# Sparse attention as one stream of steps: later PV products, an earlier compressed branch, top-k in pieces, full-height masks

## The reference

```python
# compressed branch: 127 compressed keys; its probabilities also rate the 32 blocks of 64 keys
s_c = einsum('btgrd,bngd->bgrtn', q_g, k_cmp) * ATTN_SCALE
p_c = _masked_softmax(s_c, end_pos <= pos)
o_c = einsum('bgrtn,bngd->btgrd', p_c, v_cmp)
imp = einsum('bgtn,nj->bgtj', sum(p_c, axis=2), overlap)
score = where(forced, inf, where(causal, imp, -inf))
sel_val, sel_idx = top_k(score, 16)       # 16 of 32 blocks for each query and group
# selected branch: softmax over the keys of the chosen blocks; window branch: the last 512 keys
o = g[..., 0:1] * o_c + g[..., 1:2] * o_s + g[..., 2:3] * o_w
# FoX: causal softmax attention with a forget bias, 16 heads
y = sigmoid(g_a) * (o_nsa @ w_up_nsa) + sigmoid(g_b) * (o_fox @ w_up_fox)
```

## Time and profile before

| what | us |
|---|---|
| median of 3 runs | 9327.44 |
| lowest and highest of them | 9312.08, 9807.5 |
| the profiled execution | 9306.09 |
| its span on the slowest core (core 5) | 9304.6 |
| spans of the 8 cores | 9266.1 to 9304.6 |
| mean granted TensorE clock of core 5 | 0.960 of full speed |
| PE busy over the span | 8538.8 |

### The profile page before, as it was taken

The page is one execution under the profiler, slowest core; times in us unless marked ns, Lnnn a source line. Parts: engine busy times, 40 slices in busy tenths (PEclk is TensorE's granted clock), DMA queues, the critical chain, the costliest instruction groups (busy, mean ns, idle before and its releaser), DMA issues.

```text
span 9304.6 us, 111637 instructions; the slowest of 8 cores (9266.1 to 9304.6 us)
## 1 busy us (share of the span) xinstructions
PE 8538.8 (92%) x42959; PEld 3887.5 (42%) x42959; DVE 1613.7 (17%) x3493; ACT 1743.1 (19%) x2961; POOL 355.5 (4%) x676
## 2 busy tenths in 40 slices
PE   1279999999998888888889999999999999999999
PEld 0134444444444543333334444444444444444444
DVE  2233113110001112222222223111101111111111
ACT  1134323221005652222220013000000000000000
POOL 0000000000000000000000000000000000000000
PEclk7589999999999999999989999999999999999999
DMA  9963678788623331222225566446545654564465
GB/s 193 171 147 80 111 127 152 146 147 150 119 55 78 83 85 39 56 53 43 52 56 114 116 153 135 81 95 152 124 77 114 151 110 75 128 154 93 77 141 126
DMA packets 334602, 1014.58 MB, mean 109 GB/s; under 512 B 81056, under 2 KB 138816, under 8 KB 248832
## 3 DMA queue, kind: packets, MB, share of 16 engines
q0 software_dynamic: 96768, 700.33, 42.8%
q1 hardware_dynamic: 237312, 307.10, 10.2%
HBM read 1573.38 MB, written 134.22 MB: 184 GB/s over the span
## 4 chain that ended last, share of the span: by engine, by line
PE 85%; DMA 6%; DVE 4%; issue 2%; ACT 2%; DVEq 0%; SPq 0%; ACTq 0%; POOLq 0%
PE ps L339 84%; DMA xt_25_67<-xT 1%; DMA ws_43<-w_ada 1%; DMA ws_46<-w_ada 1%; DMA xt_26_68<-xT 1%; PE ps L343 1%; DMA xt_27_69<-xT 1%; DVE of_78_120 L353 0%; DMA cx_46_88<-xT 0%; DVE onsa_140 L359 0%; DVE oaccS_139 L353 0%; DVE oaccS_139 L359 0%; ACT pT_74_116 L346 0%; ACT pT_76_118 L346 0%; ACT pT_75_117 L346 0%
## 5 line engine op out<-in xcount | busy, mean ns | idle before, releaser
L339 PE MATMUL ps<-hown_61,ws_43 128*128 128x512 bf16 x2816 | 718.9, 392 | 3.0 <-DMA ws_43<-w_inF 3.0
L339 PE MATMUL ps<-hown_61,ws_45 128*128 128x512 bf16 x2816 | 717.6, 393 | 0.0
L339 PE MATMUL ps<-hown_61,ws_44 128*128 128x512 bf16 (+1 forms) x2688 | 690.4, 394 | 0.0
L346 ACT ACTIVATE rl_138_180<-ps 128x512 f32<-128x512 f32 x128 | 76.4, 597 | 2118.5 <-PE ps L339 2118.5
L339 PEld LDWEIGHTS ps<-hown_61,ws_45 128*128 128x128 bf16 x2816 | 265.9, 101 | 272.8 <-issue 59.3
L339 PEld LDWEIGHTS ps<-hown_61,ws_43 128*128 128x128 bf16 x2816 | 264.5, 100 | 271.8 <-issue 58.6
L339 PEld LDWEIGHTS ps<-hown_61,ws_44 128*128 128x128 bf16 (+1 forms) x2688 | 255.4, 101 | 257.5 <-issue 58.6
L339 PE MATMUL ps<-hown_61,ws_46 128*128 128x512 bf16 x1472 | 344.1, 388 | 0.0
L339 PE MATMUL ps<-x1T_164,ws_45 128*128 128x512 bf16 x1408 | 309.4, 380 | 13.1 <-DVE x_132_174 L359 13.1
L339 PE MATMUL ps<-x1T_164,ws_43 128*128 128x512 bf16 x1408 | 307.6, 379 | 0.0
L339 PE MATMUL ps<-uT_179,ws_44 128*128 128x512 bf16 x1408 | 307.5, 379 | 0.0
(11 more groups left out here) (453 smaller groups left out, 9909.1 us busy)
## 6 DMA issues: line engine op xcount, KB each, us to landing
ws_44<-w_ada POOLq DMA_DIRECT2D x53, 1024.0 KB, 10.5
ws_46<-w_ada POOLq DMA_DIRECT2D x48, 1024.0 KB, 10.7
ws_43<-w_ada POOLq DMA_DIRECT2D x46, 1024.0 KB, 10.7
ws_45<-w_ada POOLq DMA_DIRECT2D x45, 1024.0 KB, 11.5
ws_43<-w_inF POOLq DMA_DIRECT2D x44, 1024.0 KB, 9.0
ws_45<-w_inF POOLq DMA_DIRECT2D x44, 1024.0 KB, 8.5
ws_45<-w_ff POOLq DMA_DIRECT2D x43, 1024.0 KB, 8.8
ws_43<-w_ff POOLq DMA_DIRECT2D x43, 1024.0 KB, 9.7
```

Source lines behind the costliest of these rows:

```text
L339: S.emit(PE, lambda e: e.matmul(out_, lhsT, rhs, start=start, stop=stop, skip_group_check=True), reads, writes)
L346: S.emit(ACT, lambda e: e.activation(out=out_, in_=in_, func=func, **kw), reads, writes)
```

## The change

All three branches of a group become one generator of steps, `group(g)`, and one loop drives it. In each step the loop writes the score and mask products and the exponential, then up to three pieces from a list `todo`, then the PV of the step before last (`LAG = 2`), whichever branch that step belongs to, and at a branch's end its work on DVE (`post`). The compressed branch of the next tile stands between the window and the selected branch of this one. The eight top-k operations, the transpose to `selT` and its copy, and the transposes of `onsa` wait in `todo`. `selT` has 128 rows (96 of them zero), as have the compressed keys, so every mask product contracts over 128 partitions. `FILL_N` gives 430 ns of GEMM to a step, and 1000 (window, selected) or 2200 (compressed) plus another 430 after a branch's last PV. There are two `oacc` tiles, four `pq` tiles and two `selT` tiles; the next 256 queries are loaded two tiles ahead. In FoX `fin` is put back by one more step. The transposes go to bank 7 of PSUM instead of bank 4, and the modulation work that used this bank is drained before the stage. The total of products is the same but for the height of the masks. In the diff, cut to its core, the `post` shown is that of the compressed branch, and the last `todo.extend` is that of the selected one, whose `out_` transposes `onsa`; the NSA lines that these replace stand in the kernel above.

```diff
-                    pend.append(fin)
+                    pend.append(lambda: pend.append(fin))
...
+            def scores(s_, n, k, kb, q4, masks):
+                out_ = s_.t[:, 0:4 * n].rearrange("p (r t) -> p r t", r=4)
+                mm(out_, k, q4[0], True, not masks, [kb, q4[1]], [s_.b])
+                for i, (a, b, rd) in enumerate(masks):
+                    mm(out_, a, rep4(b), False, i == len(masks) - 1, rd, [s_.b])
...
+                def post():
+                    smt = weights(n, q0, g, 0)
+                    oa = oacc[q0] = oar.next()
+                    for r in range(4):
+                        p, c0 = oap(r)
+                        if r == 0:
+                            ts(DVE, imp.t[0:n], p.t[0:n, c0 + 129:c0 + 161], smt.t[0:n, 4:5], None, ALU.mult, None,
+                               [smt.b], [imp.b, p.b])
+                        else:
+                            stt(imp.t[0:n], p.t[0:n, c0 + 129:c0 + 161], smt.t[0:n, 4 + r:5 + r], imp.t[0:n],
+                                ALU.mult, ALU.add, [smt.b], [imp.b, p.b])
+                        ts(DVE, oa.t[0:n, r, :], p.t[0:n, c0:c0 + 128], smt.t[0:n, r:r + 1], None, ALU.mult, None,
+                           [smt.b], [oa.b, p.b])
+                    j = 32 * QT.index((q0, n))
+                    sT = selT[q0] = selTs.next()
+                    todo.extend([
+                        lambda: tt(DVE, sc.t[0:n], imp.t[0:n], ftab.t[0:n, j:j + 32], ALU.add, [imp.b, ftab.b], [sc.b]),
...
+                        None, None,
+                        lambda: tr(PtB[0:32, 512:512 + n], sbb.t[0:n, 0:32], ident[0:n, 0:n], [sbb.b, cb.b], [Pt.b]),
+                        lambda: cp(DVE, sT.t[0:32, 0:n], PtB[0:32, 512:512 + n], [], [sT.b, Pt.b]),
+                        lambda: ready.add(q0)])
+                    return 2200
...
+                    todo.extend([None] * 5 + [out_])
...
+            load_q(0)
+            yield from comp(*QT[0])
+            for i, qt in enumerate(QT):
+                for j, (t0, _) in enumerate(QL):
+                    if t0 == qt[0]:
+                        load_q(j + 1)
+                yield from window(*qt)
+                if i + 1 < len(QT):
+                    yield from comp(*QT[i + 1])
+                else:
+                    yield None
+                yield from selected(*qt)
...
+                    s_, pT = Rst.next(), pq.next()
+                    s(s_)
...
+                run_todo(3)
+                if len(pend) > LAG or (step == "end" and pend):
+                    pv, pT, post = pend.pop(0)
+                    pv(pT)
+                    if post is not None:
+                        yield FILL_N + (post() or 1000)
+                yield FILL_N
```

More of the change, by code:

```diff
@@ L19 @@
 QOFF = NK - TOWN
+QT = [(128 * i, 128) for i in range(8)]
+QL = [(256 * i, 256) for i in range(4)]
 SCALE = 128 ** -0.5
@@ L977, in nsa @@
         kwT = ZN.tile("kwT", [128, NK], BF16)
[L978 removed]
+        ZN = Bump(M, o_misc, o_aend)
         ca = ZN.tile("ca", [128, NCA], BF16)
[L980 to L982 removed]
+        ftab = ZN.tile("ftab", [128, 32 * len(QT)], F32)
+        vs = ZN.tile("vs", [128, NK // 128, 130], BF16)
+        vw = ZN.tile("vw", [128, NK // 128, 130], BF16)
         q4r = ZN.ring("q4", 2, [128, 4, 256], BF16)
[L984 to L985 removed]
+        pq = ZN.ring("pq", 4, [128, 512], BF16)
+        oar = ZN.ring("oacc", 2, [128, 4, 128], F32)
         onsa = ZN.tile("onsa", [128, 4, 128], BF16)
[L987 removed]
+        smr = ZN.ring("sm", 4, [128, 12], F32)
         imp = ZN.tile("imp", [128, 32], F32)
@@ L995, in nsa @@
         sbb = ZN.tile("sbb", [128, 32], BF16)
-        selT = ZN.tile("selT", [32, 128], BF16)
+        selTs = ZN.ring("selT", 2, [128, 128], BF16)
         dma(POOL, ca.t[:], ca_d, [], [ca.b])
         dma(SP, ftab.t[:], ftab_d, [], [ftab.b])
-        memset(vs.t[:, :, 128:130], 1.0, vs.b)
-        memset(vw.t[:, :, 128:130], 1.0, vw.b)
+        for v in (vs, vw):
+            memset(v.t[:, :, 128:130], 1.0, v.b)
+        for v in selTs.items:
+            memset(v.t[:], 0.0, v.b)
         memset(vcmp.t[:, :, 128:129], 1.0, vcmp.b)
@@ L1002, in nsa @@
         cp(DVE, vcmp.t[:, :, 129:161], rep4(ca.t[:, CA_OV:CA_OV + 32]), [ca.b], [vcmp.b])
-        cmpb = ca.t[:, CA_CMPB:CA_CMPB + 1024]
         Rst = Ring(PS[0:2])
         OA = PS[2:4]
[L1006 to L1013, removed]
+        Pt = PS[7]
+        PtB = PSB[id(Pt)]
+        LAG = 2
@@ L1014, in weights, with oap @@
+        todo = []
+        def oap(r):
+            return OA[r // 2], 256 * (r % 2)
+        def weights(n, q0, g, br):
+            smt = smr.next()
             for b in range(2):
-                ts(DVE, smt.t[:, 8 + 2 * b:10 + 2 * b], OA[b].t[:, 128:385:256], 1e-30, None, ALU.max, None, [],
+                ts(DVE, smt.t[0:n, 8 + 2 * b:10 + 2 * b], OA[b].t[0:n, 128:385:256], 1e-30, None, ALU.max, None, [],
                    [smt.b, OA[b].b])
-            recip(smt.t[:, 4:8], smt.t[:, 8:12], [], [smt.b])
+            recip(smt.t[0:n, 4:8], smt.t[0:n, 8:12], [], [smt.b])
@@ L1018, in weights, with pv4 @@
             c = 12 * g + br
-            tt(DVE, smt.t[:, 0:4], smt.t[:, 4:8], gate_tok.t[:, qt, c:c + 10:3], ALU.mult, [gate_tok.b], [smt.b])
+            tt(DVE, smt.t[0:n, 0:4], smt.t[0:n, 4:8], gate_tok.t[0:n, QT.index((q0, n)), c:c + 10:3], ALU.mult,
+               [gate_tok.b], [smt.b])
             return smt
-        def pv4(pT, v, kt, first, last, np_=128, ncol=129):
+        def pv4(pT, n, v, vb, first, last, ncol=129):
             for r in range(4):
                 p, c0 = oap(r)
-                mm(p.t[:, c0:c0 + ncol], pT.t[0:np_, 128 * r:128 * r + 128], v, first and r % 2 == 0, last,
-                   [pT.b, kt], [p.b])
+                mm(p.t[0:n, c0:c0 + ncol], pT.t[:, n * r:n * r + n], v, first and r % 2 == 0, last, [pT.b, vb], [p.b])
@@ L1028, in nsa, with run_todo @@
+        def run_todo(k):
+            while todo and k:
+                f = todo.pop(0)
+                k -= 1
+                if f is not None:
+                    f()
         for g in range(4):
@@ L1032, in nsa @@
             dma(SP, vs.t[:, :, 0:128], d_vs[g], g_vs[g], [vs.b])
[L1033 to L1055, removed]
-                    else:
[L1057 to L1123, removed]
-                   PmB[:, 0:512].rearrange("p (j t) -> p j t", j=4), [],
-                   [b for r in range(4) for b in rbs(oT, 4 * g + r, 128 * qt, 128)] + [Pm.b])
@@ new lines, in nsa @@
+            first = True
+            pend = []
+            steps = group(g)
+            while True:
+                step = next(steps, "end")
+                if step is None:
+                    run_todo(99)
+                    continue
+                if first:
+                    yield 14000
+                    first = False
+                if step != "end":
+                    s, bias, pv, post, n = step
+                    s_, pT = Rst.next(), pq.next()
+                    s(s_)
+                    if bias is None:
+                        act(pT.t[:, 0:4 * n], s_.t[:, 0:4 * n], AF.Exp, [], [pT.b, s_.b], scale=SCALE)
+                    else:
+                        act(pT.t[:, 0:4 * n], s_.t[:, 0:4 * n], AF.Exp, [cf.b], [pT.b, s_.b], scale=SCALE, bias=bias)
+                    pend.append((pv, pT, post))
+                elif not pend and not todo:
+                    break
+                run_todo(3)
[5 more added lines that the diff above has]
+                yield FILL_N
```

74 lines of the change are left out of this document (72 added, 2 removed).

## The result

The changed kernel takes 8943.68 us (median of 4 runs, 8932.69 to 9208.56). The ratio is **0.9593, 95% interval 0.9565 to 0.962**, 4.1% faster. The forecast was 8995 us, 3.6% faster. The time lies in the range and the sign held, but the gain was under-forecast: the interval leaves the forecast's own ratio, 0.964, outside. The profiled execution is now 8932.7 us, 373 us less than the one before, against a sum of 327.

A forecast was written before the change was run, and what follows sets the result against it. PE was taken as the bound, losing time to waits, half clock and mask gaps. Savings of 76 + 130 + 100 + 21 = 327 us from 9306.1 gave 8979, or 8995 us for the median; range 8895 to 9110.

The forecast's parts named there:

- waits term: NSA stage: PE's 225 us without a product, mostly waits for DVE, fall to about 95, saving 130 us.
- Masks, 76 us: Selected steps: 128-row masks shrink two gaps from 0.31 to 0.216 us at each of 400 masks, saving 76 us.
- 60 to 100 that I set out as a sign: NSA branch ends: 96 waits before each branch's first PV, 0.5 to 1 us each, 60 to 100 us in all.
- Clock, 100 us: NSA stage: of 115 us lost to half clock, 100 come back, as falls follow no wait as short as those left.
- FoX, 21 us: FoX: PE's 42.8 us of waits for `of` lose 21 with one more step between; sixteen head ends keep theirs.
- At the end, 0: Behind the attention: some 80 us of gate products run there, as dense as any, so 0 us gained or lost.
- rival of DVE's chain: Three branch ends cost about 1.75 us each and let the clock fall: median 9162 us, chance 12%.
- slower rival: NSA steps with two GEMM products are too thin and all run at half clock: median 9575 us, chance 3%.

The follow-up runs named there:

- e2: The changed kernel with the selected masks contracting over 32 partitions again instead of 128: 9007.8 us (a second run 9050.6).
- e1: The kernel before with only selT made 128 rows tall (96 zero), so selected masks contract over 128 partitions: 9193 us.
- e12: The kernel of e1 (the kernel before with 128-row selected masks alone) run once more: ratio 0.9883 to the kernel before.
- e7: The changed kernel with the accumulators OA in a ring of three banks: ratio 0.954 to the kernel before.
- e4: The changed kernel without the GEMM products that follow a branch's last PV: ratio 0.9889 to the kernel before, 9203 us at best.
- e5: The changed kernel with no GEMM products in its steps, those behind a branch's last PV kept, masks of 128 rows: 8967.9 us.
- e6: As e5, no GEMM products in the changed kernel's steps, but with 32-row masks: ratio 0.9704 to the kernel before, 9020 us at best.
- e9: The kernel of e7 with FoX's last PV, normalisation and transposes carried into the next head's steps: ratio 0.9508 to the kernel before.
- e11: The kernel of e9 with FoX's PV two steps behind its scores and six pT tiles: ratio 0.9428 to the kernel before, 8789 us at best.

## Why the prediction's direction held, and which of its steps failed

The step that failed is the size of the waits term: 130 us forecast, 164 measured, and that is 34 of the 46 us by which the sum fell short. A second step failed beside it: the prediction let the clock hang on the waits alone and gave the masks no part in it, though by themselves they bring back 48 of the 114 us that half speed cost.

- *Masks, 76 us.* Right as the price of the gaps: 75 to 78 us (e2). What failed is the step that left the masks out of the clock: taken alone they gave 109 to 113 us (e1, e12).
- *Waits, 130 us.* The place and the cause were right: one set of banks, waits only at the three ends (e7), which cost 1.9 to 2.6 us each where the cover is missing (e4). The size failed: 225 us fell to 60, not 95, so 164. I took a mean of 8.7 GEMM products behind window and selected ends; the order, shown ahead of the prediction, has 10 behind each window end and 8 behind each selected end, since 430 ns is so close to the 427 of two products that the counts repeat. With 10 the sum for the window end is 0.7 - 0.28 = 0.4 us, against 0.36 on average. For the selected end I took 0.9, and it is 0.84; for the compressed end 0.7, and it is 0.51. In all 1.7 us a tile instead of 2.3, and loads and the rest 7 us instead of 20. The 53 us at the ends also lie below the 60 to 100 that I set out as a sign.
- *Clock, 100 us.* All of it came back, 114 to 2 us. The step that failed is the cause, not the sum: 48 us of the 114 go with the masks alone, the rest with the waits, and in the changed kernel the two removals overlap (113 us for the masks when they come first, 75 when they come last).
- *FoX, 21 us.* Over the whole of FoX the wait for `of` fell from 44.4 to 21.1 us, about as worked out, but 5.4 us came back as waits for ACT, which I had not looked for; FoX is 17.9 us shorter. No run undoes this part by itself.
- *At the end, 0.* Right: 80 us of gate products at a clock of 1.00.

From FoX's last transposes to the up projection, 1408.8 us became 1057.1. Of these 352 us, 163 are time without a product, 110 half speed, and 79 are left for the gaps at the masks; with FoX's 18 that is 370 of the 373 us. The rival of DVE's chain did not occur; that ends of this length bring the clock down was right (e4). The slower rival was unfounded: its row showed steps behind a fall, with short masks, not steps that fall by themselves (e1, e5, e6). The Trainium skill's rule on 32 rows (TensorE: Matmul & The Clock Gate, "Why this matters for your kernels") would have left 75 us out; the Trainium skill's TensorEngine Tiling (Array Packing), "Key Properties", by which a change of the tiling mode drains the engine, agrees with the 75 us of e2.

## What to carry to other kernels

When accumulators are shared by successive branches, what pays is independent work behind each branch's last product, long enough for the emptying chain, or one more bank; the new order by itself only moved the wait (e4); the lag of a product behind its exponential counts only where the trace shows PE waiting for it, as FoX did and NSA did not. Count the filler from the order written out, not from its mean. Keep small masks at full height when they sit between full-height products: the gaps are in the starts of the rows, not among the waits.

## What the runs showed of the hardware

- A 32-row product between 128-row ones put about 0.1 us on either side of it, 75 to 78 us for 400 of them (e2).
- A wait of 1.5 to 2 us was accompanied or followed by 1.2 GHz in 14 of 21 cases with 32-row masks in the steps around it, and in 6 of 40 with 128-row masks at the same places (e1, e12). Tall masks are no guard where such waits stand close together: in e4 it was 19 of 19. Without long waits the clock held in both forms, even in steps without any dense GEMM (e5, e6).
- A list of waits can understate what they cost: 33 us of listed waits in FoX, 140 of at most 0.3 us, were worth 65 us of the stage (e9, e11). PE's busy time there fell from 515 to 485 us for the same 4034 products, so some 30 us of it had been waiting.
